# Another order in the prologue of a two-block transformer kernel, and products in TensorE's pauses

## The reference

```python
mod_x = adaln_params(c, ada_w[l], ada_b[l])          # silu(cond) @ w + b, for x and for ctx
hx = modulate(rms_norm(x, norm_mix_g[l]), mod_x[:, 0], mod_x[:, 1])
...
qkv = silu(centred_depthwise_conv(p_qkv, conv_w))    # 5 taps
q = l2_normalize(q) * HEAD_DIM ** -0.5; k = l2_normalize(k)
beta = sigmoid(dirs(p_beta))
g = -exp(a_log) * softplus(dirs(p_a) + dt_bias)
o_f, s_f = gated_delta_chunked(q, k, v, g[0], beta[0], s_init[0])   # cumsum of g, exp of differences
...
hid = silu(t @ w1) * (t @ w3); out += (hid * gate) @ w2             # mixture of 32 experts, top 2 of one group
```

## Time and profile before

| | |
|---|---|
| median of 3 runs | 1745.18 us (1744.93 to 1747.8) |
| profiled execution, time | 1752.4 us |
| profiled execution, span | 1750.7 us |
| PE busy | 1620.0 us (93%) |
| mean granted clock | 0.96 |
| chain of work that ended last | PE 76%, DMA 10%, DVE 9% |

### The profile page before, as it was taken

The page is one execution under the profiler, slowest core; times in us unless marked ns, Lnnn a source line. Parts: engine busy times, 40 slices in busy tenths (PEclk is TensorE's granted clock), DMA queues, the critical chain, the costliest instruction groups (busy, mean ns, idle before and its releaser), DMA issues.

```text
span 1750.7 us, 21577 instructions
## 1 busy us (share of the span) xinstructions
PE 1620.0 (93%) x8397; PEld 1042.1 (60%) x8397; DVE 550.6 (31%) x1122; ACT 331.0 (19%) x667; POOL 173.3 (10%) x178
## 2 busy tenths in 40 slices
PE   5999999999999979989988989998799999999986
PEld 2576676676588868875544569756534544443433
DVE  2456766666520011144211120283511111011002
ACT  2443233343231100020100021241200000000001
POOL 1334433334300000000000000000000000000000
PEclk8899999999999987979999999899899999999998
DMA  9511111011844422437999994202299999999993
GB/s 367 220 49 36 48 36 48 24 48 36 342 151 145 152 88 96 167 121 289 407 421 421 420 390 150 73 0 101 98 409 421 421 407 422 420 422 398 422 421 132
DMA packets 58861, 404.40 MB, mean 231 GB/s; under 512 B 6766, under 2 KB 6898, under 8 KB 12576
## 3 DMA queue, kind: packets, MB, share of 16 engines
q1 hardware_dynamic: 52704, 381.92, 54.3%
q0 software_dynamic: 6080, 21.39, 4.0%
HBM read 402.19 MB, written 1.10 MB: 230 GB/s over the span
## 4 chain that ended last, share of the span: by engine, by line
PE 76%; DMA 10%; DVE 9%; issue 2%; ACT 1%; SPq 1%; DVEq 0%; POOL 0%; ACTq 0%; POOLq 0%
PE bank L648 75%; DMA ring<-in_moe 6%; DVE arena L1667 3%; DMA arena<-in_moe 2%; DMA ring<-in_dense 2%; ACT arena L1320 1%; PE bank L1076 1%; DVE arena L1722 1%; DVE arena L1738 1%; DVE arena L1727 0%; DVE arena L1719 0%; DVE arena L1717 0%; DVE arena L1731 0%; SPq L489 0%; SPq L478 0%
## 5 line engine op out<-in xcount | busy, mean ns | idle before, releaser
L648 PE MATMUL bank<-arena 128*128 128x128 f32 (+4 forms) x3032 | 501.3, 315 | 28.4 <-DVE arena L1741 6.8
L648 PEld LDWEIGHTS bank<-arena 128*128 128x128 f32 (+3 forms) x3032 | 400.1, 190 | 149.0 <-issue 53.1
L648 PE MATMUL bank<-ring,arena 128*64 128x512 f32 (+2 forms) x1608 | 461.6, 605 | 24.1 <-DMA ring<-in_moe 17.0
L1320 ACT ACTIVATE arena<-bank 128x256 f32<-128x256 f32 (+1 forms) x372 | 166.0, 452 | 1148.9 <-PE bank L648 868.1
L648 PEld LDWEIGHTS bank<-ring,arena 128*64 128x64 f32 (+2 forms) x1608 | 144.2, 138 | 243.9 <-issue 239.7
L648 PE MATMUL bank<-hc,head_w 128*128 128x512 f32 (+1 forms) x384 | 164.4, 534 | 0.0
L2056 DVE TENSOR_TENSOR arena<-arena,bank 128x256 f32<-128x256 f32 x48 | 20.2, 422 | 344.5 <-ACT arena L1320 344.5
L648 PE MATMUL bank<-arena,ring 128*128 128x256 f32 x416 | 94.8, 386 | 1.8 <-DVE arena L1833 1.2
L648 PE MATMUL bank<-hc,ring 128*128 128x256 f32 x416 | 90.4, 379 | 0.0
L648 PEld LDWEIGHTS bank<-arena,ring 128*128 128x128 f32 x416 | 80.6, 194 | 13.8 <-DVE arena L1833 1.6
L648 PE MATMUL bank<-o_heads,arena 128*64 128x512 f32 (+2 forms) x184 | 87.2, 619 | 1.3 <-DMA ring<-in_moe 1.3
(11 more groups left out here) (263 smaller groups left out, 1306.2 us busy)
## 6 DMA issues: line engine op xcount, KB each, us to landing
ring<-in_moe SPq DMA_DIRECT2D x201, 1024.0 KB, 17.2
ring<-in_dense SPq DMA_DIRECT2D x62, 1024.0 KB, 7.6
o_heads<-in_moe SPq DMA_DIRECT2D x23, 1024.0 KB, 17.8
xc<-in_moe SPq DMA_DIRECT2D x22, 1024.0 KB, 16.5
arena<-in_moe SPq DMA_DIRECT2D x21, 1024.0 KB, 19.0
hc<-in_moe SPq DMA_DIRECT2D x21, 1024.0 KB, 17.2
head_w<-in_head_w POOLq DMA_DIRECT2D x27, 512.0 KB, 3.9
xc<-in_dense SPq DMA_DIRECT2D x7, 1024.0 KB, 6.0
```

The costliest lines, as they stand in the source:

```text
L648: return nc.tensor.matmul(out, lhsT, rhs_, start=start, stop=stop, **kw)
L1320: return nc.scalar.activation(out, in_, func, **kw)
```

## The change

Some loads wait: the second part of the constants and parts 1 and 2 of head 0's weights are issued when slot 6 has landed. Beta is made as 1 / (1 + exp(-x)), the exponential on ACT, addition and reciprocal on VectorE; exp(a_log) and the table load come ahead of ACT's first copy of a projection. GpSimd masks beta ahead of the decay stores. VectorE does two taps of part 0 ahead of g and three after it, and the taps of part 1 ahead of waiting for the cumulative exponentials. ACT makes these exponentials ahead of the two copies of decay rows, and `activate(0, 0)` and `activate(0, 1)` ahead of `decay_sizes(0)`. PE does two of the eight products of part 2 ahead of the sums of g. Last, `keep_warm(n)` issues n products of 512 columns whose result nobody reads: five in the first adaLN round, two at each of three places in each router and mixture, one ahead of and one behind the third norm's sums, two ahead of the projection after attention, and one ahead of each variance: 23 in all.

```diff
                 if g == KT:
+                    sp.wait_ge(landed[HOME[KT - 2]], LANDED_AT[KT - 2])
...
             load_part(0, 0)
-            pool.wait_ge(s["rnorm"], 1)
+            pool.wait_ge(landed[HOME[KT - 2]], LANDED_AT[KT - 2])
...
             load_part(1, 0)
-            for d in range(2):
-                pool.wait_ge(s["decay_turned"], d + 1)
-                pool.dma_start(decay_dram[HEADS * d:HEADS * (d + 1), :], decay_T[d][0:HEADS, :]).then_inc(s["rows_stored"], 16)
...
+            pool.wait_ge(s["mats_landed"], 16)
+            pool.wait_ge(s["beta_made"], 1)
+            mask_beta(0)
+            for d in range(2):
+                pool.wait_ge(s["decay_turned"], d + 1)
+                pool.dma_start(decay_dram[HEADS * d:HEADS * (d + 1), :], decay_T[d][0:HEADS, :]).then_inc(s["rows_stored"], 16)
...
-            pool.wait_ge(s["mats_landed"], 16)
-            pool.wait_ge(s["gates_acted"], 1)
-            mask_beta(0)
...
+            def keep_warm(n):
...
+                for _ in range(n):
+                    mm(bank[7][:, :], ones[:, :], mats[:, 0:4, :].rearrange("p a b -> p (a b)"))
...
                 ada_step(0, k)
+                if k >= 3:
+                    keep_warm(1)
...
+            project_head(0, 2 * KT, 2)
...
                 mm(bank[(7, 3)[d]][:, :], ones[0:1, :], decay_T[d][0:1, :]).then_inc(s["gate_sums"], 1)
-            project_head(0, 2 * KT, KT)
+            project_head(0, 2 * KT + 2, KT - 2)
...
+                keep_warm(2)
                 pe.wait_ge(s["router_landed"], 16 * (m + 1))
...
+                keep_warm(2)
                 pe.wait_ge(s["kept"], m + 1)
...
+                keep_warm(2)
                 pe.wait_ge(s["rows_copied"], 4 * (m + 1))
...
             mixture(0)
+            keep_warm(1)
...
                 norm_sum(1, k)
+            keep_warm(1)
...
+                keep_warm(1)
                 for k in range(KT):
...
+            keep_warm(2)
             pe.wait_ge(s["heads_rnorm"], 8)
...
             act.wait_ge(s["pads_zeroed"], 3)
+            act_fn(gd["kb"][:, 0, :], V("a_log"), ACT.Exp).then_inc(s["gates_acted"], 1)
+            log_and_exp()
...
             act.wait_ge(s["gates_made"], 1)
-            act_fn(gd["beta"][:, :, :], gates_in[:, :, 0:DH], ACT.Sigmoid).then_inc(s["gates_acted"], 1)
-            log_and_exp()
...
             act_fn(gd["t"][:, :, :], gd["t"][:, :, :], ACT.Ln, bias=eps_ap[1.0]).then_inc(s["gates_acted"], 1)
-            act_fn(gd["kb"][:, 0, :], V("a_log"), ACT.Exp).then_inc(s["gates_acted"], 1)
+            act_fn(gd["beta"][:, :, :], gates_in[:, :, 0:DH], ACT.Exp, scale=-1.0).then_inc(s["gates_acted"], 1)
...
                 act_fn(decay_T[d][0:HEADS, :], bank[2 * d][0:HEADS, :], ACT.Copy).then_inc(s["decay_turned"], 1)
+            act.wait_ge(s["gates_made"], 3)
+            act_fn(gd["t"][:, :, :], gd["G"][:, :, :], ACT.Exp).then_inc(s["cum_exp"], 1)
+            act_fn(gd["kd"][:, :, :], gd["kd"][:, :, :], ACT.Exp).then_inc(s["cum_exp"], 1)
...
                 act_fn(flat(decay_rows[d]), bank[(7, 3)[d]][:, :], ACT.Copy).then_inc(s["decay_turned"], 1)
-            act.wait_ge(s["gates_made"], 3)
-            act_fn(gd["t"][:, :, :], gd["G"][:, :, :], ACT.Exp).then_inc(s["cum_exp"], 1)
-            act_fn(gd["kd"][:, :, :], gd["kd"][:, :, :], ACT.Exp).then_inc(s["cum_exp"], 1)
...
-            decay_sizes(0)
...
             activate(0, 1)
+            decay_sizes(0)
...
             tt_(gates_in[:, :, DH:2 * DH], ba[:, :, DH:2 * DH], times(V("dt_bias"), TT), ALU.add).then_inc(s["gates_made"], 1)
-            conv_taps(0, 0, 0, CONV - 1)
+            conv_taps(0, 0, 0, 2)
             dve.wait_ge(s["gates_made"], 1)
-            dve.wait_ge(s["gates_acted"], 3)
+            dve.wait_ge(s["gates_acted"], 2)
...
                 ).then_inc(s["gates_made"], 1)
-            conv_taps(0, 0, CONV - 1, CONV)
+            dve.wait_ge(s["gates_acted"], 3)
+            link(ts_(gd["beta"][:, :, :], gd["beta"][:, :, :], 1.0, None, ALU.add))
+            nc.vector.reciprocal(gd["beta"][:, :, :], gd["beta"][:, :, :]).then_inc(s["beta_made"], 1)
+            conv_taps(0, 0, 2, CONV)
...
                 ).then_inc(s["gates_made"], 1)
+            conv_taps(0, 1, 0, CONV)
             dve.wait_ge(s["cum_exp"], 2)
-            dve.wait_ge(s["gates_acted"], 1)
+            dve.wait_ge(s["beta_made"], 1)
...
-            conv_taps(0, 1, 0, CONV)
```

## The result

The changed kernel takes 1729.99 us (median of 4 runs, 1725.48 to 1731.75) where the kernel before takes 1746.49 us beside it (4 runs, 1744.93 to 1751.51): a ratio of 0.9898, 95% interval [0.9877, 0.9919]. It is faster, by 16.5 us. Forecast were 20.4 us (to 1724.8), with 1715 to 1736 as the range, which holds it.

The account below looks back on a forecast made before the run. PE's chain of work was taken as the bound, so earlier mixtures reach the end: 8.8 + 4.5 + 3.8 + 1.6 + 1.7 = 20.4 us off 1752.4, less 7.2 for the runs' median, gives 1724.8; range 1715 to 1736.

Parts of the forecast that it names:

- rival (c): Prologue keeps little, head 0 at half clock or its stores landing late: 4 instead of 8.8, 1729.6 us; chance 0.12.
- (b): Added products don't hold the clock at the routers: 0 there in place of 8.3, 1733.1 us; chance 0.2.
- Prologue, 8.8: All work up to head 0's first products comes 8.8 us earlier, bounds 6 and 10.5.
- Held back, both slots should land by about 30.5: adaLN round: delaying 1.9 MB of other loads, 4.5 us, lets slots 6 and 7 land before PE waits for them.
- 0.86: adaLN round: eight steps and four added products at 0.86 us each, 10.3 us, ending at 34.05 instead of 35.34.
- Beta and the early products, 1.6 less 1.2: Before g's sums: beta without sigmoid gains 1.6 us; two early third-projection products delay the sums by 1.2.
- Decays, 9.8: Head 0: earlier decay stores and reordered activations end its pair of exponentials 9.8 us earlier, at 63.8..64.3 instead of 73.89.
- The mask beside the taps: Prologue: GpSimd's mask of beta, 2.06 us, lies beside three of VectorE's convolution taps, which is not free.
- Head 0: New PE pause of about 2.5 us before head 0's first real work; charged 1 us, ends 0 and 3.
- Router 1, 4.5: Up to mixture 1: added products hold the clock in logits and gather; 4.5 us, bounds 1 and 5.4.
- Router 2, 3.8: Up to mixture 2: the same clock gain with less slack; 3.8 us, bounds 0 and 5.
- Projection after attention and last variance, 1.6 and 1.7: Added products in pauses of 2.6 and 1.9 us keep full clock: 1.6 and 1.7 us, bounds 0 and 1.7 each.

Follow-up runs that it names:

- the prologue alone: The changed kernel without the 18 added products outside the prologue, keeping the prologue's five; 1739.27 us, ratio 0.9961 against the kernel before.
- the products alone: The kernel before with only the 18 added products of routers, norms and projection after attention; 1736.01 us, ratio 0.9943.
- The order alone: The changed kernel with no added product at all, keeping held loads, new order, new beta and two early projection products; 1738.83 us, ratio 0.9963.

## Why the prediction was right

Right were the direction, the range, and the reason why a gain reaches the end: the 12.7 us at mixture 1's first product are 12.8 at attention's. The sum, 20.4 us, stands against 19.3 in the traces with attention's and mixture 2's own variation taken off, and against 16.5 by the medians. The 16.5 is nearer to rival (c), by which the prologue keeps 4 and the whole gains 15.6, than to the forecast, and its interval (14.1 to 21.5) holds both. What speaks against (c) is the prologue alone, 7.4 us with 4.5 as its lower end, and the head loop's end: 486.60 to 487.39 in the four traces with the changed prologue, 493.71 and 493.86 in the two with the old one. Against (b) speak the gathers, which held full clock, and the 10.6 us of the products alone. That the sum comes so near is in part luck: the prologue gave 1.7 less than forecast and router 1 about 1 more.

**Prologue, 8.8: measured 7.1 in the trace, 7.4 by itself.** The size was right, its shares were not. The failed step is "Held back, both slots should land by about 30.5". Transfers of 4.5 us were not what step 7 was late by: with the loads held back and nothing added it still waited, and started at 31.76 instead of 33.41, 1.65 us earlier. Two slots then land 2.49 us apart, which is 1 MB at 421 GB/s, and no slice of rows 1 moves more than 422: I take the stream itself as the limit. Issued as before beside the added products, the loads cost 0.79 us of waiting. The step that mis-sized the products is "0.86" for each of twelve pieces: alternating with the narrow steps a pair takes 2.05. The round took 11.85 us where the sum had 10.3, and that its end was only 0.3 us off the forecast's 34.05 is luck, for it had begun 1.3 us early. What the products cost in the round they give back in transposes, bias product and projection (from 36 to 43 us before, all at a granted clock of 0.50), and no more. I had counted both edits as if each brought its own part; either does nearly alone what the two do.

**Beta and the early products, 1.6 less 1.2.** Both had the forecast's size where they act: g was ready at 50.50 (forecast 49.85), with 1.6 us of the gain from beta, and the early products delay the sums by 1.1 us (28.1 against 29.2 from the first step). But the early products hide most of what beta wins, the mask of beta hides most of their own delay, and neither edit moved the first products of head 0 by more than 0.3 us. The step that failed is crediting 1.6 us through to the exponentials: at the sums only 0.5 of it is left, at head 0's first products 0.1.

**Decays, 9.8: measured 8.1.** The mechanism was right. 4.9 us come through the stores, which are issued earlier, and 3.3 us because silu and squares of both parts lie in the landing instead of behind the differences. The second share is read from the two traces; no run put that order back by itself. The order alone, with held loads and without any added product, keeps 7.6 of the 8.1 us (65.16 against 72.74).

**The mask beside the taps.** By my sum the taps beside the mask cost nothing, having a microsecond in hand. Three took 3.53 us against 2.25 at the 0.75 each of a tap alone, and the mask 2.78 against 2.06: both engines lost. The work of the two, 4.31 us alone, was done in 3.56 (51.11 to 54.67), so they did overlap. The sums were taken 3.4 us after their start, as forecast (4.5 less 1.1). The delay on the taps was 1.3 us, with no semaphore between them and the mask: the engines did not meet at semaphores alone.

**Head 0.** The pause came as forecast, at 3.67 us instead of 2.5, and about the 1 us charged was lost: 8.1 at the exponentials, 7.7 at the first products, 7.1 behind the loop. The last 0.6 to 0.7 is the clock's fall: the stage table separates the four traces in which it fell from the ten in which it didn't. In the prologue-alone trace the third projection ran at half clock in part (8.45 us for its 12 entries instead of 5.42), which filled the pause down to 0.42 us; the clock was up again for head 0, and the loop ended at the same 486.76 although the first step had started 0.8 us later. PE's row of that kernel:

```profile
57.33 8.45 PE L650 MATMUL bank<-hc,head_w 128*128 128x512 f32 x12
```

**Router 1, 4.5: measured 4.9 (from the logits' start to mixture 1, 25.7 to 20.8 us), 5.6 from the loop's end, and 3.8 with the products alone.** The doubt that I had halved the gain for was real: the clock falls in the middle of the logits. But it decides nothing: the kernels in which it held through the logits reach mixture 1 no sooner after the loop (289.8 to 290.2 us) than those in which it fell (289.7 to 289.8), for they had lost as much ahead of the logits. The forecast's 2.8 us at the logits take them at about 3.9 us instead of 6.89, less 0.2 for the two products ahead of them, and no run shows 3.9: it was my estimate from a gather of as many entries, 3.74. In the kernel before the granted clock was 0.52 from 763.5 to 770 us, in the logits, and 0.53 from 781.8 to 788, in the gather; where it held through the logits of router 1, they took 3.76 to 3.79. Over the eleven profiled kernels with a pair ahead of them the logits of router 1 took 3.76 to 4.86 us and held full clock in four; at router 2 3.75 in five and 5.28 to 5.73 in six. The gathers held in 21 of 22.

**Router 2, 3.8: measured 3.1**, and 5.1 in the run with the products alone, where the clock held through the logits.

**Transposes.** The forecast added nothing for the pair behind the transposes, since in the row of before the clock rose right behind them. The pair took 2.65 us at router 1 (at full 1.88) and 1.88 at router 2. Without that pair the clock stayed at half from the transposes' end at 764.5 beyond 770 us (0.50), where before it rose right behind the same sixteen (1.00 from 774), and at router 2 of the changed kernel it rose at 1226.0 us (0.50 in the microsecond ahead, 1.00 in the one behind), while the last transposes still ran. One row of before was too little to forecast from; the runs show both.

**Projection after attention and last variance, 1.6 and 1.7**: 7.17 instead of 8.86 and 3.72 instead of 5.41, 1.7 each. In the two experiments without these products the last variance took 3.72 once and 5.41 once, so a part of executions has nothing to gain there.

## What to carry to other kernels

Edits that lead to the same meeting point don't add up: here held loads and added products each did nearly alone what both did, and two early products hid most of what the new beta won. A store's landing hides nothing that holds back the store itself; what it can hide is work put beside it, here 3.3 us. A product without use paid where the work behind it then kept the clock (gather 3.81 us instead of 6.59, projection 7.17 instead of 8.86, variance 3.72 instead of 5.41), and little where that work lost it again (gating, back at 0.50 after 3 us). Compare the lengths of stages, not whole times or bare starts, when single edits are worth one or two microseconds: the clock elsewhere moved the total by six, and the start of untouched work by nearly two.

## What the runs showed of the hardware

- TensorE fell from full clock although it was never idle: logits of 36 columns fell 2.6 us after their start, those of 16 columns 1.4 us after theirs, and gating products of 128 columns, alternating with products over one row, 3 us after theirs, though nine products of 512 columns had run just ahead. The logits fall in some executions and not in others of nearly the same kernel. It isn't the columns alone: behind the head loop 64 entries of 128 columns kept the clock at 1.00.
- Attention, untouched, took 67.3 to 73.3 us from its first product to the sums behind it, over all profiled runs (73.2 or more in four, 67.3 to 70.3 in ten), with the granted clock of its 25 us stretches between 0.73 and 1.00. Most of the scatter of the whole times lies there.
- A 128x512 product between adaLN steps of 32 columns takes 1.0 to 1.1 us, where in a row of its like it takes 0.86 to 0.89.
- The two stores of 16 KB each, issued by GpSimd while the loads ran at some 420 GB/s, kept it waiting 4.7 to 5.9 us in the nine traces of the new order where the differences wait for them.
- The reciprocal of 128x64 takes 0.55 us on VectorE, an addition of that size 0.19 to 0.22.
